# A hybrid decoder layer on one core: weights ahead of the feed-forward part split once and kept in DRAM, block loop written out, last rows scaled into four tiles

## What is computed

```python
def _layer(x, ...):
    u = _rmsnorm(x, g_mix)
    z = u @ w_in + b_in
    q, k, v, xb, yb = jnp.split(z, [Q_END, K_END, V_END, X_END], axis=-1)
    attn, nk, nv = _attn_prompt(q, k, v, attn_sinks)      # sliding window of 128, 8 heads of 64
    xc, nconv = _causal_conv(xb, conv_prefix, conv_w, conv_b)
    lru, nh = _rg_lru(xc, h0, w_a, b_a, w_i, b_i, lam)    # recurrence, width 512
    mix = jnp.concatenate([attn, lru * jax.nn.gelu(yb)], axis=-1)
    h = x + mix @ w_out + b_out
    gate, up = jnp.split(_rmsnorm(h, g_ffn) @ w_ffn_in, [D_FF], axis=-1)   # D_FF = 2816
    y = h + (jax.nn.silu(gate) * up) @ w_ffn_out
```

## Time and profile before

| what | us |
|---|---|
| median of 3 runs | 2334.44 |
| the runs | 2334.39, 2334.44, 2338.91 |
| the profiled execution | 2338.64 |
| its span, first to last instruction | 2337.0 |

### The profile page before, as it was taken

How to read it: one execution, slowest core, us unless ns; L and a number is a source line. 1 busy time by engine, 2 the same in 40 slices (tenths; PEclk the granted TensorE clock), 3 DMA queues, 4 the chain that set the end, 5 groups by cost and what they waited for, 6 DMA issues and landing times.

```text
span 2337.0 us, 31534 instructions
## 1 busy us (share of the span) xinstructions
PE 2243.3 (96%) x12183; PEld 1892.9 (81%) x12183; DVE 1239.6 (53%) x2086; ACT 889.1 (38%) x1393; POOL 32.4 (1%) x66
## 2 busy tenths in 40 slices
PE   6999999999999999999999999999988799999997
PEld 6767888888777888888866888888877699999997
DVE  4586444446486444445577553534648554444443
ACT  4574222243385322234366322224347432222221
POOL 1000000000000000000000000000010000000000
PEclk8999999999999999999999999999999799999998
DMA  4123323322313323232312333232331122222321
GB/s 140 54 60 121 100 90 98 92 90 91 109 53 115 95 91 97 89 94 91 117 64 89 102 91 99 88 102 83 98 114 37 29 82 90 88 84 83 91 84 63
DMA packets 77019, 207.34 MB, mean 89 GB/s; under 512 B 9389, under 2 KB 25981, under 8 KB 76848
## 3 DMA queue, kind: packets, MB, share of 16 engines
q1 hardware_dynamic: 70272, 184.58, 25.6%
q0 software_dynamic: 3936, 12.03, 1.5%
q10 hardware_dynamic: 2656, 8.62, 0.9%
HBM read 196.44 MB, written 9.77 MB: 88 GB/s over the span
## 4 chain that ended last, share of the span: by engine, by line
PE 86%; DVE 7%; ACT 4%; issue 2%; DMA 1%; ACTq 0%; POOL 0%; DVEq 0%
PE bank L577 27%; PE bank L579 27%; PE bank L578 27%; PE bank L736 1%; DVE s_p L1406 1%; PE bank L713 1%; DVE xc L1443 1%; ACT w_hi L967 1%; DVE w_lo L1298 1%; PE bank L636 1%; PE bank L677 1%; PE bank L695 0%; PE bank L615 0%; PE bank L727 0%; DVE om L1471 0%
## 5 line engine op out<-in xcount | busy, mean ns | idle before, releaser
L577 PE MATMUL bank<-x_hi,w_hi 128*128 128x512 f32 (+1 forms) x2320 | 832.3, 359 | 7.3 <-DVE x_lo L1338 4.8
L579 PE MATMUL bank<-x_hi,w_lo 128*128 128x512 f32 (+1 forms) x2320 | 820.2, 354 | 0.0
L578 PE MATMUL bank<-x_lo,w_hi 128*128 128x512 f32 (+1 forms) x2320 | 819.1, 353 | 0.0
L967 ACT ACTIVATE w_hi<-w_raw 128x1024 fp32r<-128x1024 f32 (+1 forms) x360 | 374.0, 1039 | 1078.7 <-PE bank L579 1061.3
L1298 DVE TENSOR_TENSOR w_lo<-w_raw,w_hi 128x1024 fp32r<-128x1024 f32 (+1 forms) x360 | 432.0, 1200 | 214.1 <-ACT w_hi L967 211.1
L577 PEld LDWEIGHTS bank<-x_hi,w_hi 128*128 128x128 f32 x2320 | 439.0, 189 | 83.9 <-issue 17.7
L578 PEld LDWEIGHTS bank<-x_lo,w_hi 128*128 128x128 f32 x2320 | 439.4, 189 | 63.7 <-issue 4.4
L579 PEld LDWEIGHTS bank<-x_hi,w_lo 128*128 128x128 f32 x2320 | 438.5, 189 | 60.9
L577 PE MATMUL bank<-a_hi,w_hi 128*128 128x512 f32 (+1 forms) x1200 | 425.6, 355 | 15.5 <-DVE w_lo L1298 7.4
L579 PE MATMUL bank<-a_hi,w_lo 128*128 128x512 f32 (+1 forms) x1200 | 424.4, 354 | 0.0
L578 PE MATMUL bank<-a_lo,w_hi 128*128 128x512 f32 (+1 forms) x1200 | 423.8, 353 | 0.0
(11 more groups left out here) (269 smaller groups left out, 1393.6 us busy)
## 6 DMA issues: line engine op xcount, KB each, us to landing
w_raw<-in_units SPq DMA_DIRECT2D x264, 512.0 KB, 3.5
w_raw<-in_units SPq DMA_DIRECT2D x64, 448.0 KB, 3.3
x_tok<-in_x_prompt POOLq DMA_DIRECT2D x16, 512.0 KB, 5.9
w_raw<-in_units SPq DMA_DIRECT2D x32, 256.0 KB, 2.6
w_raw<-in_units SPq DMA_DIRECT2D x128, 64.0 KB, 2.5
out_y_p<-y_tok ACTq DMA_DIRECT2D x16, 512.0 KB, 2.6
gfin<-in_g_fin POOLq DMA_DIRECT2D x1, 512.0 KB, 6.8
kc_tok<-in_cache_k POOLq DMA_DIRECT2D x1, 512.0 KB, 5.0
```

The source lines that it names most:

```text
L577: nc.tensor.matmul(out, h, hi[:, kt, c0:c1], start=(first and kt == kts[0]), stop=False)
L578: nc.tensor.matmul(out, h, lo[:, kt, c0:c1], start=False, stop=False)
L579: mm = nc.tensor.matmul(out, l, hi[:, kt, c0:c1], start=False, stop=(kt == kt_of[u] - 1))
L967: w_hi_ready.by(A(w_hi[:, u % RING, 0:n], w_raw[:, u % RAW, 0:n], ACT.Copy))
```

## The change

It has three parts.

1. In block 0 all units are loaded raw and split as before, and SP also stores both parts of units 0 to 21 into a DRAM tensor (`keep`). In blocks 1 to 3 these 22 units (KEEP) are not split: SP loads the two parts straight into the slots of `w_hi` and `w_lo`, or, for every fourth unit, into a slot laid over the two raw slots (`w_kept`). The feed-forward units are handled as before.
2. The loops over blocks 0 to 2 on PE, ACT, DVE, POOL and SP are written out, so that waits compare with constants.
3. After block 3, the prompt rows are scaled into the four parts of `x_tok`, not into the two of `y_tok`; PE transposes the third quarter and the sample rows into other banks, and DVE takes the sample rows second.

The core of the diff:

```diff
+        def is_kept(b, u):
+            return b + u // NU >= 1 and u % NU < KEEP
+        def slot(b, u):
+            b, u = b + u // NU, u % NU
+            if u >= KEEP or b == 0:
+                return (u + b) % RING
+            if u == KEEP - 1:
+                return slot(b, u - 3)
+            return ((b - 1) % RING, RING, b % RING, (b + 1) % RING)[u % 4]
...
+            def store_parts(u):
+                sp.wait_ge(w_ready, u + 1)
+                sp.dma_start(keep[u, 0], w_hi[:, u % RING, :].bitcast(F32)).then_inc(kept_out[u % RING], 16)
+                sp.dma_start(keep[u, 1], w_lo[:, u % RING, :].bitcast(F32)).then_inc(kept_out[u % RING], 16)
+            def load_parts(b, u):
+                if u == 1:
+                    sp.wait_ge(w_ready, splits_before(b, 0))
+                elif u < 4:
+                    gemm_done.wait(sp, b, (-2, None, -1, 0)[u])
+                elif u == KEEP - 1:
+                    gemm_done.wait(sp, b, u - 3 + 1)
+                else:
+                    gemm_done.wait(sp, b, u - 4 + 1)
+                landed = kept_in[slot(b, u)]
+                hi, lo = parts(b, u)
+                sp.dma_start(hi.bitcast(F32), keep[u, 0]).then_inc(landed, 16)
+                sp.dma_start(lo.bitcast(F32), keep[u, 1]).then_inc(landed, 16)
+            for u in range(NU):
+                load_raw(0, u)
+                if RAW <= u < KEEP + RAW:
+                    store_parts(u - RAW)
+            for b in range(1, NB):
+                for u in range(KEEP):
+                    load_parts(b, u)
+                for u in range(KEEP, NU):
+                    load_raw(b, u)
...
-            with pe.Fori(0, NB - 1) as b:
+            for b in range(NB - 1):
...
             freed.wait(pe, NB - 1, NU - UO0)
             y_T(NB - 1, 0)
+            y_stat(NB - 1, True)
             y_T(NB - 1, 1)
-            y_stat(NB - 1, True)
-            y_T(NB - 1, 2)
-            y_T(NB - 1, 3)
-            y_ready.wait(pe, NB - 1, 3)
+            y_T(NB - 1, 2, (G[0], G[1]))
+            stdy_ready.wait(pe, NB - 1, 1)
...
+            y_ready.wait(pe, NB - 1, 1)
+            y_T(NB - 1, 3, S)
...
             def split(b, u, end=False):
-                if end and u >= NU:
+                if end and u >= NU or is_kept(b, u):
                     return
...
                 unit_done(act, b, u - RING)
+                if b == 0 and RING <= u < KEEP + RING:
+                    act.wait_ge(kept_out[u % RING], stored(u - RING))
...
+            y_scale(b, 0, S, x_tok[:, 0, :])
...
+            for m, o in ((1, TB), (2, (G[0], G[1])), (3, S)):
+                y_scale(b, m, o, x_tok[:, m, :])
```

More of the change, by code:

```diff
@@ L295, in hymba_layer @@
         transfers = [1 + NKV * 2 if u in U_O else 1 for u in range(NU)]
[L296 to L299, removed]
+        raw_in = [sem(f"raw_in{i}") for i in range(RAW)]
+        w_hi_ready = sem("w_hi_ready")
+        w_ready = sem("w_ready")
+        kept_out = [sem(f"kept_out{i}") for i in range(RING)]
+        kept_in = [sem(f"kept_in{i}") for i in range(RING + 1)]
         gemm_done = Signal(sem("gemm_done"), NU)
@@ L429, in _, with load_raw @@
         def _(sp):
[L430 to L439, removed]
+            def load_raw(b, u):
+                n = splits_before(b, u)
+                if n >= RAW:
+                    sp.wait_ge(w_ready, n - RAW + 1)
+                if b > 0 and KEEP <= u < KEEP + RAW:
+                    gemm_done.wait(sp, b, RAW_LAST + 1)
+                n = kt_of[u] * P
+                raw, src, landed = w_raw[:, u % RAW, :], units[u], raw_in[u % RAW]
+                if u not in U_O:
+                    sp.dma_start(raw[:, 0:n], src[:, 0:n]).then_inc(landed, 16)
                     return
-                landed.by(sp.dma_start(raw[:, JT * P:n], src[:, JT * P:n]))
+                sp.dma_start(raw[:, JT * P:n], src[:, JT * P:n]).then_inc(landed, 16)
                 for g in range(NKV):
@@ L1264, in _ @@
             chain.restart()
-            with act.Fori(0, NB - 1) as b:
+            for b in range(NB - 1):
                 mixers(b, False)
@@ L1754, in _ @@
             chain.restart()
-            with dve.Fori(0, NB - 1) as b:
+            for b in range(NB - 1):
                 mixers(b, False)
@@ L1763, in _ @@
             y_rstd(b, True)
+            y_scale(b, 0, S, x_tok[:, 0, :])
             dve.wait_ge(state_out, 16 * N_STATE_OUT)
[L1766 to L1767 removed]
             dve.wait_ge(smp_pe, 8)
[L1769 removed]
             for h in range(2):
[L1771 removed]
+                ins = STT(out=y_tok[0:NS, 0, h * 512:(h + 1) * 512], in0=(G[2], V)[h][0:NS, :],
                           scalar=rstd_t[0:NS, QB:QB + 1], in1=gfin[0:NS, h * 512:(h + 1) * 512],
```

97 lines of the change are left out of this document (59 added, 38 removed).

## The result

| | before | changed |
|---|---|---|
| median, first measurement (5 runs each) | 2334.44 | 2323.60 |
| lowest and highest | 2333.34, 2338.91 | 2317.46, 2326.67 |
| ratio, 95% interval | | 0.9946 [0.9928, 0.9964] |
| profiled execution, its span | 2338.64, 2337.0 | 2317.46, 2315.5 |

What follows compares the result with a forecast made beforehand. PE was busy for 96% of the span, so only its idle rest and slow matmuls could be won. Terms 10.4 + 5.3 + 4.4 + 1.2 + 3.2 = 24.5 us off 2334.44 gave 2309.9 us, range 2303 to 2317 (0.64).

Steps and rivals of the forecast that it cites:

- the written-out loop: Start of the mixers: no jump wait in blocks 1 and 2, earlier first softmax, shorter `sd` wait; 5.3 us less.
- the wait for `sd` in block 3: Block 3's mixers: without splits by DVE and ACT before the first softmax, PE's 4.5 us wait shrinks by 2.0 us.
- The splits: Mixers of blocks 1 and 2: PE's waits for `w_lo`, `pT` and `ii` end, 5.2 us per block, 10.4 us.
- the lower bound: Jump removal at the mixers: 3.6 us less what the `sd` chain takes back, 0 if it starts from DVE.
- The clock's 1.2 us: Block 1's mixers: 10 matmuls after the jump wait ran at clock 0.51, taking 1.2 us too long.
- Block 3: Block 3's mixers: splits removed from three long PE waits, 4.4 us less, plus 1.2 us from a shorter slow-clock stretch.
- The clock's term: Block 3's mixers: a shorter lower-clock stretch behind a shortened wait, 1.2 us; bounds nothing and half of 43 us.
- What it costs: Kept loads in blocks 1 to 3, block 0's added stores and more code: all hidden, cost nothing.
- The end: After block 3: the last store lands earlier through the new scaling order, 3.2 us gained, within 2.2 to 4.4.
- Rival 1: PE's waits pass from DVE to ACT, next in the chain; only 8.5 us won, 2326 us; chance 0.08.
- Rivals 3 to 5: Transfers slightly late, 2315 to 2321 us (0.10 beyond 2317); queue held for landing times, 2348 (0.06); nothing in sum, 2330 to 2339 (0.04).

Runs made afterwards that it cites:

- `loops`: Kernel before with only the five hardware loops written out, every split and the old tail kept: 2334.85 us, ratio 1.0003.
- `loops`, wait moved: Kernel before with loops written out, splits kept, and ACT's wait for the y stores put behind the first exponentials: 2326.39 us, ratio 0.9969.
- the wait moved: Changed kernel with ACT's wait for the head's last y stores put behind the first exponentials: 2309.00 us, measured again 2311.10 us.
- `tail`: Kernel before with only the new ending: last rows into four tiles, sample rows second; 2333.65 us, ratio 0.9995.
- with the exponential ahead as well: Changed kernel with ACT's store wait behind the first exponentials and a one-column exponential at the head of ACT's mixers: 2310.19 us, ratio 0.9897.
- SP waits: Changed kernel with SP waiting, before it loads unit 9 in blocks 1 to 3, until the y rows have landed: 2311.37 us, ratio 0.9903.
- exponential ahead only: Changed kernel with a one-column exponential at the head of ACT's mixers, its store wait left in place: 2317.64 us, ratio 0.9939.

## Why the prediction was wrong

Two steps failed. One is that the written-out loop would bring the first softmax and `sd` forward: the jump went, but the wait for `sd` rose by 2.0 and 1.4 us in blocks 1 and 2, in each 1.4 of it through a table load that the straight code put behind `sd`. The other is the wait for `sd` in block 3, counted 2.0 us shorter, with nothing set down for the stores on ACT: it became 0.9 to 1.2 us longer. Between the means of the two pairs of profiles PE's idle time fell by 13.0 us, between the medians the time fell by 10.8 and 14.1 us.

**The splits (10.4 us): right.** Idle time from `loops` to the changed kernel falls by 5.7 + 4.9 us, in the second profile by 5.4 + 5.0. From `loops`, wait moved to the wait moved it falls by 5.2 in each block, the forecast number. The wrong part was the working: I gave ACT 0.4 us of it.

**The written-out loop (5.3 us): measured 0.8 to 1.0 in idle time and nothing in the median.** The failed step is "the first softmax is earlier and the wait for `sd` in block 2 should fall". It rose to 2.8 us in `loops`, in both blocks. I had written down the lower bound, 0 "if that chain starts from DVE and not from PE", and not followed the chain. With the wait moved, which takes the table load out of it, `sd` is 1.4 us and idle time in blocks 1 and 2 is 3.6 us under the mean of before: most of the 2.2 + 1.4 + 0.5 us forecast was there, and the load took 2.7 of it. The clock's 1.2 us in it was the luck of one execution: the second profile of before has no slow stretch in block 1.

**Block 3 (4.4 us and 1.2 of clock): measured about 1 in idle time (0.6 between the means of the two pairs of profiles, 1.3 against `loops`).** The two waits for `pT` fell by 1.2 and 1.1 us, as forecast. The wait for `sd`, for which I took 2.0, rose by 0.9 to 1.2. That I tied to ACT's split of unit 8; PE waited at the end of a chain of table load, exponentials, `xb`, convolution and softmax, and ahead of it stood the stores. The clock's term is open: PE's busy time in this stage fell from 164.9 and 165.3 us to 162.4 in both profiles, more than 1.2, but in `tail`, which changes nothing there, it was 161.8.

**What it costs (0): a cost of 1.1, 1.9 and 3.0 us on ACT, in which the kept loads were never late for PE.** I asked of each new transfer only when its own reader needs it. The store that shares the 16 engines with it has a reader as well, ACT, and the change itself took 1.9 us of that reader's cover by the splits alone. The working for the kept loads was too pessimistic: `w_hi` and `w_lo` landed 3.2 and 4.1 us after issue, a pair 4.5 us after its first issue, not 5.3. Block 0 did not become longer: 145.2 and 145.0 us for its mixers and out-projection, 145.2 and 143.6 before.

**The end (3.2 us): measured 2.2, and 0.8 alone.** In the timeline after, from DVE's first scaling at 2298.57 to the span's end at 2315.5 there are 16.9 us; before 19.1.

```profile
2297.77 1.97 PE L717 MATMUL bank<-ident,hT 128*128 128x128 f32 x16
...
2298.57 1.41 DVE L1453 SCALAR_TENSOR_TENSOR x_tok<-bank,rstd_t,gfin 128x512 f32<-128x512 f32 x2
...
2300.01 6.42 ACTq L1126 DMA_DIRECT2D out_y_p<-x_tok  x4
...
2300.72 1.40 DVE L1855 SCALAR_TENSOR_TENSOR y_tok<-bank,rstd_t,gfin 32x512 f32<-32x512 f32 x2 [0.74 <-PE bank L1017]
2302.04 4.02 DVE L1453 SCALAR_TENSOR_TENSOR x_tok<-bank,rstd_t,gfin 128x512 f32<-128x512 f32 x6
```

Scaling takes 7.5 us, within the forecast. From the last issue's end to the span's end there are 9.1 us in place of 7.2 for the small stores: 1.9 more, where I had allowed 0.6 to 1.4. In `tail` DVE waits longer; PE's transposes took 3.60 us there for 16 and not 1.97, and the mean granted clock from 2308 to 2312 us was 0.57, against 1.00 from 2297.7 to 2301 us after:

```profile
2308.04 3.60 PE L637 MATMUL bank<-ident,hT 128*128 128x128 f32 x16
...
2312.62 1.40 DVE L1772 SCALAR_TENSOR_TENSOR y_tok<-bank,rstd_t,gfin 32x512 f32<-32x512 f32 x2 [2.37 <-PE bank L937]
```

**The rivals.** Rival 1, waits passed on to the next in the chain, was right for the jumps and wrong for the splits, for which I had made it. Rivals 3 to 5 looked at transfers late for PE; the longest wait for one was 0.2 us. The forecast time, 2309.9, is what the version with the wait moved reaches; that is luck in part, since by its terms there is more clock in it and less at the end and in block 3.

## The clock

The mean clock decides several us, and the wait ahead of block 3's gates goes with it in most kernels. Windows of block 3's mixers and out-projection in before, its second profile, the changed kernel, the wait moved, and `loops` with the wait moved:

```profile
1718.95:1909.87 190.92, 164.86 (x1180) 146.76 (x1179) 123.37 (x325) 100.40 (x210) 8.11 (x16) 0.89 0.18 54
```
```profile
1714.98:1905.03 190.05, 165.26 (x1180) 147.49 (x1179) 123.36 (x325) 100.37 (x210) 8.11 (x16) 0.89 0.18 54
```
```profile
1705.36:1892.51 187.15, 162.44 (x1181) 144.46 (x1179) 107.56 (x311) 87.26 (x196) 8.07 (x16) 0.91 0.27 95
```
```profile
1700.43:1884.92 184.49, 161.43 (x1180) 144.04 (x1179) 107.58 (x311) 87.32 (x196) 8.11 (x16) 0.92 0.28 97
```
```profile
1713.41:1899.86 186.45, 160.67 (x1181) 143.74 (x1180) 123.28 (x325) 100.24 (x210) 8.07 (x16) 0.92 0.18 55
```

The longest single wait for `sd` in block 3 and the mean clocks of the runs, side by side: `loops` with the wait moved 2.5 us, 0.986 to 0.987; the wait moved 3.0 and 2.0, 0.986 to 0.988; with the exponential ahead as well 2.0, 0.985 to 0.988; SP waits 3.4, 0.987; exponential ahead only 3.6, 0.983 to 0.987; before and `loops` 3.8, 0.981 to 0.986; changed 4.7 and 5.0, 0.982 to 0.985. This was not tested by itself: I made no kernel that lengthens that wait alone, and `tail`, with a wait of 3.8 us, had 0.984 to 0.987. That the clock is part of the gain is measured; that this one wait is why is argued. The rest is the execution's: before block 0's mixers the same instructions kept PE busy for 51.8 us at a mean clock of 0.88 in one profile of before and for 49.6 at 0.90 in the other. The Trainium skill, TensorE: Matmul & The Clock Gate, section What's actually happening, has the gate run on a phase that the program does not set, so that equal kernels get different numbers of slow matmuls; these two profiles agree.

## What to carry to other kernels

When a change frees an engine at the head of a chain, follow that chain to its end, instruction by instruction, and list every wait on it, also those that had never ended last: their cover shrinks by what was freed. Ask of every added transfer which older transfers it shares the DMA engines with, and who waits for those. Put a wait next to the first instruction that needs it, and keep slack waits away from an instruction that brings a table load. When a loop is written out, look again at which side of a wait such a load stands. Before two traces are compared, set each against the spread of its own kernel's runs.

## What was not expected of the hardware

- Writing out a loop on five engines removed a wait of 1.4 to 2.2 us per turn and changed the time by 0.0003 of it, with an interval of 0.001 on either side; it also moved a table load of 1.28 us on ACT from before `sd` to behind it.
- A 512 KB store landed in 4.8, 5.6 and 6.7 us beside 1 MB of loads issued in the same moment, and in 2.6, 4.7 and 5.3 us at the same places with these loads held back. The 4.7 us hold 1.85 us in which a 16 KB packet of the instruction queue was under way and after which the last sixteenth of the store began.
- Moving one wait on ACT by five instructions won 8.5 us in `loops` and 9 to 11 us in the changed kernel, about half of it clock.
- Four 512 KB stores in a row at the end need 9.1 us from the last issue to the end of the span, against 7.2 us for small ones.
